# A hybrid attention and delta-rule step on one core: the last projection pieces, six loads and two VectorE products change places

## What is computed

```python
h = rms_norm(x, norm_mix)
proj = h @ w_in
...
fox_out = fox_attention(fq, k_all, v_all, cum[:, p_len:], cum, pos[p_len:], pos)
qkv_c, new_gdn_ctx = causal_depthwise_conv(qkv, gdn_ctx, w_gdn_conv)
qkv_c = jax.nn.silu(qkv_c)
...
o, new_s = gated_delta_chunked(cq, ck, cv, g, beta, s0)
o = rms_norm(o, gdn_out_norm) * jax.nn.silu(gz.reshape(b, t, GDN_HEADS, GDN_HEAD_DIM).astype(f32))
mix = jnp.concatenate([fox_out.reshape(b, t, FOX_WIDTH), o.reshape(b, t, GDN_WIDTH).astype(x.dtype)], axis=-1)
x = x + mix @ w_out
...
x = x + (jax.nn.silu(gate_c) * up) @ w_down
```

## Time and profile before

| what | value |
|---|---|
| median of 3 runs | 1809.84 us (1804.15 to 1815.65) |
| profiled execution, its own time | 1811.04 us |
| its span | 1809.5 us |
| busy PE / DVE / ACT / POOL | 1663.9 / 955.6 / 687.6 / 521.0 us |
| mean granted PE clock | 0.951 of full speed |
| moved by DMA | 156.04 MB, 86 GB/s over the span |

### The profile page before, as it was taken

One profiled execution on the slowest core, in us unless ns is written; L12 is line 12 of the kernel. 1 busy time (PEld: TensorE's weight loads), 2 busy tenths in 40 slices (PEclk: granted clock), 3 DMA queues, 4 the chain that ended last, 5 costly groups with the idle time before them and its releaser, 6 DMA issues. The chain is left out here.

```text
span 1809.5 us, 30580 instructions
## 1 busy us (share of the span) xinstructions
PE 1663.9 (92%) x10991; PEld 1571.9 (87%) x10991; DVE 955.6 (53%) x1711; ACT 687.6 (38%) x1085; POOL 521.0 (29%) x301
## 2 busy tenths in 40 slices
PE   6998998998997658988969999999999999999998
PEld 6897787797795547978959999999999999999998
DVE  4537558658648754364255554444444444545344
ACT  5424634634534532243253332222222222445344
POOL 5113323333232106234112222222222223445441
PEclk9999998999997869989979999999999999999999
DMA  5344443344343282003024311111111111211122
GB/s 155 105 118 109 126 147 104 107 148 122 100 141 107 78 311 79 1 18 114 1 92 147 101 41 47 47 47 47 47 47 47 47 47 47 111 48 51 44 65 95
DMA packets 213892, 156.04 MB, mean 86 GB/s; under 512 B 23617, under 2 KB 202721, under 8 KB 212848
## 3 DMA queue, kind: packets, MB, share of 16 engines
q1 hardware_dynamic: 168204, 117.85, 21.4%
q10 hardware_dynamic: 45064, 36.68, 6.5%
q0 software_dynamic: 512, 0.07, 0.1%
HBM read 122.90 MB, written 31.83 MB: 86 GB/s over the span
## 5 line engine op out<-in xcount | busy, mean ns | idle before, releaser
L207 PE MATMUL ps<-x_hi,w_hi 128*128 128x344 f32 x1584 | 508.3, 321 | 1.1 <-issue 1.1
L208 PE MATMUL ps<-x_lo,w_hi 128*128 128x344 f32 x1584 | 505.6, 319 | 0.0
L209 PE MATMUL ps<-x_hi,w_lo 128*128 128x344 f32 x1584 | 505.6, 319 | 0.0
L207 PEld LDWEIGHTS ps<-x_hi,w_hi 128*128 128x128 f32 x1584 | 297.6, 188 | 3.0 <-issue 1.4
L209 PEld LDWEIGHTS ps<-x_hi,w_lo 128*128 128x128 f32 x1584 | 298.0, 188 | 0.0
L208 PEld LDWEIGHTS ps<-x_lo,w_hi 128*128 128x128 f32 x1584 | 297.3, 188 | 0.1
L207 PE MATMUL ps<-h_hi,wm_hi 128*128 128x344 f32 x672 | 227.1, 338 | 1.6 <-ACT sqr L1188 1.0
L208 PE MATMUL ps<-h_lo,wm_hi 128*128 128x344 f32 x672 | 217.6, 324 | 0.0
L209 PE MATMUL ps<-h_hi,wm_lo 128*128 128x344 f32 x672 | 217.0, 323 | 0.0
L2423 POOL TENSOR_TENSOR w_lo<-w_raw,w_hi 128x1024 fp32r<-128x1024 f32 x42 | 110.0, 2619 | 371.2 <-ACT w_hi L2591 371.2
L2770 DVE TENSOR_TENSOR x_lo<-ffn_act,x_hi 128x2064 fp32r<-128x2064 f32 x36 | 87.1, 2420 | 122.9 <-ACT x_hi L2646 122.8
(11 more groups left out here) (408 smaller groups left out, 2916.1 us busy)
## 6 DMA issues: line engine op xcount, KB each, us to landing
w_raw<-in_w_up SPq DMA_DIRECT2D x44, 512.0 KB, 4.0
k_past<-in_cache_k SPq DMA_DIRECT2D x256, 64.0 KB, 1.9
v_past<-in_cache_v SPq DMA_DIRECT2D x256, 64.0 KB, 2.0
wm_raw<-in_w_in ACTq DMA_DIRECT2D x28, 512.0 KB, 4.2
w_raw<-in_w_down SPq DMA_DIRECT2D x44, 256.0 KB, 2.7
gdn_scratch<-conv ACTq DMA_DIRECT2D x12, 528.0 KB, 3.3
xT<-x_scratch SPq DMA_DIRECT2D x1, 4128.0 KB, 13.4
x_scratch<-xT SPq DMA_DIRECT2D x8, 516.0 KB
```

Source lines behind the costliest of these rows:

```text
L207: pe.matmul(out, w_hi, a_hi, start=first, stop=False)
L208: pe.matmul(out, w_hi, a_lo, start=False, stop=False)
L209: return pe.matmul(out, w_lo, a_hi, start=False, stop=last)
```

## The change

Four edits. Tile 27 loses its own places, and stands at (3, "b"), (4, "a"), (4, "b") as in other steps; its SiLU and store go back into slot 5. The six loads of queries, states and z of heads 0 and 1 leave `load_first_pair`, and stand at the head of SP's program in `gdn`. In pair 0, `decay_queries` of head 0 stands ahead of both first inverses. At the end of each pair the output is first multiplied by weight and z, and then by the inverse norm.

```diff
-LATE_PLACE = ((5, "b"), (6, "a"), (6, "c"))
...
-            if n == NTILES - 1:
-                slot, pos = LATE_PLACE[k % NG]
...
-                for h in range(PAIR):
-                    sp.dma_start(first.qkv[h][:, 0], v.gdn_dram[h, 0]).then_inc(first.q_loaded[h], 16)
-                    sp.dma_start(blocks(first.s_dec[h]), t["state_gdn"][0, :, h:h + 1].rearrange("b a k e -> k (b a) e")).then_inc(first.s_loaded[h], 16)
-                    sp.dma_start(first.z_silu[h], v.gdn_dram[h, 3][:, 0:TOK]).then_inc(first.z_loaded[h], 16)
...
-                    if j < STEPS - 1:
-                        silu_z()
+                    z = ext[:, 1, TAPS - 1:TAPS - 1 + TOK]
+                    act.activation(z, z, ACT.Silu).then_inc(conv_silu.sem, 1)
                     square(j, 1)
-                    need(act, conv_silu, j, 1)
+                    need(act, conv_silu, j, 2)
                     store(j, 2, conv[:, 2])
-                    if j < STEPS - 1:
-                        store_z(j)
+                    store(j, 3, z)
...
-                if j == STEPS:
-                    silu_z()
-                    store_z(j - 1)
...
+            for s, h in heads(0):
+                load_rest(s, h)
             for s, h in heads(1):
                 load_first(s, h)
...
-            for s, h in heads(0):
-                first_inverse(0, s, h)
-            for s, h in heads(0):
-                decay_queries(0, s, h)
+            decay_queries(0, 0, 0)
+            first_inverse(0, 0, 0)
+            first_inverse(0, 1, 1)
+            decay_queries(0, 1, 1)
...
+                for s, h in heads(pair):
+                    need(dve, z_loaded[h], 0, 16)
+                    need(dve, osq_ready[s], pair, 1)
+                    dve.scalar_tensor_tensor(out=oT[s], in0=oT[s], scalar=v.out_norm[:], in1=z_silu[h], op0=ALU.mult, op1=ALU.mult)
                 if pair == 0:
                     for s, h in heads(1):
                         decode_inputs(1, s, h)
+                dve.drain()
                 for s, h in heads(pair):
-                    need(dve, z_loaded[h], 0, 16)
                     need(dve, orstd_ready[s], pair, 1)
-                    dve.scalar_tensor_tensor(out=oT[s], in0=oT[s], scalar=v.out_norm[:], in1=o_rstd[pair][s], op0=ALU.mult, op1=ALU.mult)
-                for s, h in heads(pair):
-                    dve.drain()
-                    dve.tensor_tensor(oT[s], oT[s], z_silu[h], ALU.mult).then_inc(o_ready[s].sem, 1)
+                    dve.tensor_tensor(oT[s], oT[s], o_rstd[pair][s], ALU.mult).then_inc(o_ready[s].sem, 1)
```

More of the change, by code:

```diff
@@ L1287, in prologue @@
                     store(j - 1, 1, conv[:, 1])
[L1289 to L1296, removed]
             def slot(j, i):
```

## The result

| | before | after |
|---|---|---|
| median | 1813.47 us (7 runs, 1804.15 to 1817.20) | 1799.50 us (7 runs, 1794.96 to 1804.26) |
| profiled execution, its own time | 1811.04 us | 1799.50 us |
| its span | 1809.5 us | 1797.9 us |

The ratio is 0.9928, with a 95% interval of 0.9908 to 0.9949: the change makes the kernel 0.7% faster. By the bound of the prediction that is "within 1%". The forecast, 1800 us against the 1809.84 us that were known then, is a ratio of 0.9946, just inside the interval.

A forecast was written before the change was run, and what follows sets the result against it. PE bounds most of the kernel, but in `fox` step 3 mostly waits for DVE. Terms -5.4 - 1.3 - 3.5 + 3.0 - 2.7 = -9.9 us against 1811.04 give 1801.1; adjusted for the median, 1800 us, range 1791 to 1813.

The forecast's parts named there:

- within 1%: Whole kernel: time changes by no more than 1%, about 18 us, what a measurement can tell from no change; chance 0.82.
- Pieces of z: Step 3 of `fox`: z's late pieces leave slots 5 to 7 for PE's waits in slots 3 and 4; -5.4 us.
- The third piece's share: Place (6, "c"): ACT's wait of 3.16 us and copy of 0.46 us go, so the step's last chain moves up 3.6 us.
- The second's: Place (6, "a"), ahead of scores DVE waits for: 1.8 us back, between 0 and 3.9, as PE's clock may be lower.
- more comes back: Slot 6, step 3: PE keeps its higher clock and both DVE waits go, 9.66 us instead of 5.4; 1795.7 us, chance 0.20.
- rival of slots 3 and 4 held up: Step 3: PE stays at its lower clock, pieces take 7.7 us each and overfill its waits; 1814.6 us, chance 0.11.
- rival of a tail paced by the cached values: Slots 6 and 7: SP's loads of the last values set the pace, pieces give nothing; 1805.4 us, chance 0.13.
- SiLU and tables: End of `fox`: with z's SiLU in slot 5, no table load precedes the exponential of the decode factors; -1.3 us.
- Loads: Barrier after `fox`: with six loads moved behind it, the 4 KB store lands sooner, from 5.8 towards 2.1 us; -3.5 us.
- Queries ahead of the first inverses: Start of `gdn`: DVE and POOL take turns, first level +1.9 us later; with PE's lower clock +3.0 in all.
- some 31 us: Start of `gdn`: sign that the first level starts some 31 us after PE's first work behind the barrier, previously 27.9.
- The end of a pair: Pair 1: two of DVE's four products move into its 9.15 us idle time, -2.7 us; pair 0 gives 0.

The follow-up runs named there:

- two places freed: Kernel before with z's last pieces at (4, a), (4, b), (5, b), so (6, a) and (6, c) are freed: ratio 0.9935.
- e1: Kernel before with the first edit alone (z's three last pieces in slots 3 and 4, SiLU and store of z in slot 5): ratio 0.9939.
- inverses first: Changed kernel with its third edit undone, both first inverses ahead of both query scalings: ratio 0.9913, median 1797.09 us.
- queries by PSUM: Changed kernel, but DVE multiplies head 0's queries by products in PSUM instead of decay rows in SBUF, leaving out their decay: ratio 0.9929.

## Why the prediction was right, and where its terms were off

**Pieces of z (-5.4).** The mechanism held: two waits of DVE for PE, one for each of two places. The third piece's share, 3.6 us by ACT's wait and copy, measured 3.52 (the offset of DVE's copy in slot 7 beside that in slot 6). The second's was the term that was mis-sized, at 1.8 us: DVE's wait fell by 3.49 us, and by the same in the run with two places freed. The 1.5 us that the weighing of slot 5 was to lose at PE's lower clock did not come: its 24 matmuls took 1.53 us in both traces. The fear was not empty, though. Of the eight traces with both places of slot 6 freed, five have 1.53 us there and a wait of 1.37; the other three (e1, inverses first, queries by PSUM) have 2.06 to 2.47 us, and waits of 1.71 to 2.13. The rival "more comes back" was right on this step. The rival of slots 3 and 4 held up failed in its first condition: with three pieces there the granted clock was 1.00 (first window after), not 0.50. The rival of a tail paced by the cached values fell with them: the decode chain moved up by 8 us. It is next in line, though: in the changed trace DVE waits 0.57 us for the last cached values (up to 1.58 us in other runs with early pieces), for which it did not wait before.

**SiLU and tables (-1.3).** The table load is worth 1.2 us (0.30 us of wait instead of 1.52 or 1.53). In the changed profile 0.38 us of it went to a wait of DVE for PE's L1103, four matmuls that ran at the lower clock there (granted 0.50; mostly 1.06 us each instead of 0.59).

**Loads (-3.5).** Landing fell by 4.4 us, to 1.4, below the 2.1 us that I took for the floor. That the six loads, and not z's own store or the eight others, held it up is shown from both sides: 1.8 us with that edit alone, 6.5 us without it alone. Behind the barrier nothing waited for the queries.

**Queries ahead of the first inverses (+3.0).** The order of turns came out as worked out: forecast 1.9 us for the stretch from the first mask to the first level, measured 1.87 to 2.03. The other part, PE's lower clock at the levels, I put at 1.1, though half of 1.9 is 0.95; and the sign "some 31 us" counts it ahead of the first level, where by the working it comes behind (27.9 + 1.9 = 29.8). The 30.35 us measured have 0.4 us of a later first mask in them, which no term held. The first level itself became 2.07 us longer in this trace, about twice the term. With this order the first level took 5.37 to 6.46 us in six kernels, with the old one 4.11 in five and 5.2 in two. So the lower clock came with this order each time, but also came without it, in two kernels where POOL's first mask came late (17.25 and 18.64 us): the order is not its only cause. Alone, the edit cost 0.16%, 2.9 us, which is barely clear of noise.

The Trainium skill's rule that I weighed there (SBUF — State Buffer, "Who interferes with whom"), that a VectorE instruction contends with a GpSimd one that reads SBUF when it has two inputs in SBUF itself, agrees with both runs: 2.87 and 3.3 us with two operands in SBUF, no delay with one of them in PSUM.

**The end of a pair (-2.7).** Measured 3.18 (9.63 to 6.45), by this edit alone 3.17. Two products fewer are 2.50 + 2.56 - 2.38 = 2.68 of it, as the term has it; the other 0.5 is mostly a start that lies closer behind the first inverse norm (0.04 us behind its end instead of 0.46), for a reason that no run settles. In pair 0 it gave nothing, as forecast: PE was 6.86 us ahead of the trace before at 761 us, in pair 0's chain, and 6.61 us at pair 1's first level.

**The sum.** -9.9 forecast, -11.5 between the two profiled executions, 14 us between the medians. The misses of the terms are of both signs and partly cancel: against the forecast the pieces with the table load gave 1.7 us more and the loads 0.9, the end of a pair 0.5, and the queries cost 1.5 us more. One stretch moved for which no term stood: the levels of pair 1 (from PE's first L1797 there, at 822.85 us before, to its last) took 49.6 us before and 48.1 after, since PE's products from 826 to 829 us ran at the lower clock before (one every 0.21 us) and their counterparts at the higher after (one every 0.11 us). They took 48.0 to 48.3 us in nine of the other traces, all four of a single edit among them, and 49.6 in two, so these runs name no edit as the cause of that 1.5 us. That the forecast of 1800 us met the median of 1799.50 is in part luck: it started from a median 3.6 us below that of the seven runs (1809.84 and 1813.47), and its gain was some 4 us too small. A part of the difference between its gain and the medians' 14 us is the profiled execution of before: its tail took 55.19 us, while the three other kernels with the same late places took 57.2 to 57.6 us. From a profile that stands 2 us low in the stretch that is to shrink, a gain is read 2 us too small.

The experiments point to the changed kernel with the old order of DVE. It ran at 0.9913 beside 0.9921 for the changed kernel on the same chip, and so beats before; that it beats the changed kernel is left open.

## What to carry to other kernels

Idle time of one engine is not a free place for an instruction, if it waits there for an engine beside which its instructions stretch (here 2.87 us instead of 1.21): look at how long they take beside that engine's in the trace, and work out the turns. Filler work for PE goes where PE waits for others, and not where others wait for PE. And a tiny store that all engines wait for can be slowed by the traffic that was queued ahead of it (here 5.8 to 6.5 us with fourteen loads, 1.4 to 2.6 with eight): loads that nobody needs yet can wait until it has landed.

## What the runs showed that I had not expected

The same instructions of `fox`'s tail differ by 2.4 us between profiled executions of kernels that are equal up to there (55.19 to 57.57). PE's clock has a part in it: the third piece, 24 equal matmuls, took 4.79 us in the trace of before and 5.41 to 5.99 in the other three. A term of 1 us from one profile is within that.
